# Second mixer of a two-block kernel: the first merge gate computed ahead of the second scan, and the scan's masked copies made by VectorE

## The reference, cut to what matters

```python
def merge_branches(gates, o_a, o_b, w_o_a, w_o_b, w_out):
    g_a, g_b = jnp.split(gates, 2, axis=-1)
    y = jax.nn.sigmoid(g_a) * (o_a @ w_o_a) + jax.nn.sigmoid(g_b) * (o_b @ w_o_b)
    return y @ w_out

def rwkv7_scan(r, w, k, v, a, b, s0):
    ...
    def step(s, inp):
        r_t, w_t, k_t, v_t, a_t, b_t = inp
        sa = jnp.einsum('...vk,...k->...v', s, a_t)
        s = s * w_t[..., None, :] + sa[..., :, None] * b_t[..., None, :] + v_t[..., :, None] * k_t[..., None, :]
        return s, jnp.einsum('...vk,...k->...v', s, r_t)
```

## Time and profile before

| | |
|---|---|
| runs | 2721.07 us median of 3 (2718.84 to 2724.94) |
| profiled execution | 2726.3 us, span from the first to the last instruction 2724.5 us |
| PE | 2413.0 us busy, 89% of the span; mean granted clock 0.946 |
| DVE, ACT, POOL | 893.3, 446.0, 85.5 us busy |
| DMA | 789.10 MB, mean 290 GB/s |

### The profile page before, as it was taken

One profiled execution on the slowest core, in us unless ns is written; L12 is line 12 of the kernel. 1 busy time (PEld: TensorE's weight loads), 2 busy tenths in 40 slices (PEclk: granted clock), 3 DMA queues, 4 the chain that ended last, 5 costly groups with the idle time before them and its releaser, 6 DMA issues. The chain is left out here.

```text
span 2724.5 us, 42972 instructions
## 1 busy us (share of the span) xinstructions
PE 2413.0 (89%) x19453; PEld 1308.2 (48%) x19453; DVE 893.3 (33%) x1682; ACT 446.0 (16%) x809; POOL 85.5 (3%) x93
## 2 busy tenths in 40 slices
PE   7999889899999999999999999896586899599985
PEld 4544343343433344434444443366576887355552
DVE  3225522303232222413141311374566521432222
ACT  3112101111111101211121201230041220000001
POOL 1001000000000000000010000000001100000000
PEclk9998879999999999999999999898797999699998
DMA  5356349999999999999999999830000033479996
GB/s 191 111 177 239 144 175 394 389 378 424 412 423 422 414 396 414 418 411 404 385 408 422 416 406 402 363 125 1 9 32 2 3 132 120 169 311 422 422 422 274
DMA packets 133522, 789.10 MB, mean 290 GB/s; under 512 B 17477, under 2 KB 27981, under 8 KB 69213
## 3 DMA queue, kind: packets, MB, share of 16 engines
q1 hardware_dynamic: 129885, 773.78, 70.3%
q0 software_dynamic: 3456, 12.58, 1.2%
HBM read 774.79 MB, written 11.53 MB: 289 GB/s over the span
## 5 line engine op out<-in xcount | busy, mean ns | idle before, releaser
L3090 PE MATMUL bank<-ring,arena 128*34 128x462 f32 (+1 forms) x3072 | 669.1, 572 | 68.0 <-DMA ring<-in_w_up 43.1
L3090 PEld LDWEIGHTS bank<-ring,arena 128*34 128x34 f32 x3072 | 175.2, 113 | 426.6 <-issue 406.3
L3113 PE MATMUL bank<-ring,arena 128*34 128x512 f32 (+1 forms) x1536 | 340.1, 559 | 0.6 <-DVE arena L2051 0.6
L3113 PEld LDWEIGHTS bank<-ring,arena 128*34 128x34 f32 x1536 | 101.7, 112 | 221.0 <-issue 203.6
L311 PE MATMUL bank<-arena,ring 128*128 128x256 f32 (+1 forms) x688 | 155.8, 388 | 3.7 <-ACT arena L1052 1.4
L311 PEld LDWEIGHTS bank<-arena,ring 128*128 128x128 f32 x688 | 131.7, 192 | 27.9 <-issue 2.0
L2044 DVE TENSOR_TENSOR arena<-arena,bank 34x462 f32<-34x462 f32 (+1 forms) x96 | 95.0, 1082 | 106.2 <-ACT arena L1121 105.9
L3569 PE MATMUL bank<-ring,arena 128*64 128x256 f32 x992 | 111.3, 380 | 6.9 <-DMA ring<-in_moe_w_up 6.1
L1121 ACT ACTIVATE arena<-bank 34x462 f32<-34x462 f32 (+1 forms) x96 | 84.9, 1038 | 121.1 <-PE bank L3090 120.9
L3569 PEld LDWEIGHTS bank<-ring,arena 128*64 128x64 f32 x992 | 73.5, 137 | 48.7 <-issue 17.0
L2988 PEld LDWEIGHTS bank<-arena 64*64 64x64 f32 x2304 | 73.1, 135 | 48.2 <-issue 47.8
(11 more groups left out here) (654 smaller groups left out, 2802.3 us busy)
## 6 DMA issues: line engine op xcount, KB each, us to landing
ring<-in_w_gate SPq DMA_DIRECT2D x128, 1408.0 KB, 13.1
ring<-in_w_up SPq DMA_DIRECT2D x128, 1408.0 KB, 12.8
ring<-in_w_down SPq DMA_DIRECT2D x128, 1408.0 KB, 10.7
ring<-in_w_in SPq DMA_DIRECT2D x47, 1024.0 KB, 7.2
ring<-in_moe_w_down SPq DMA_DIRECT2D x33, 1024.0 KB, 16.5
ring<-in_moe_w_gate SPq DMA_DIRECT2D x31, 1024.0 KB, 15.4
ring<-in_moe_w_up SPq DMA_DIRECT2D x31, 1024.0 KB, 17.9
ring<-in_ada_w SPq DMA_DIRECT2D x24, 1024.0 KB, 7.0
```

Of the source, the lines that this page charges most:

```text
L3090: last = mm(ps[c][row:row + CAP, 0:n], xsT[:, e, k, :], w[:, at:at + n], start=k == 0, stop=k == KT - 1)
L3113: last = mm(ps[6][row:row + CAP, c:c + n], hidT[:, j, :], w[:, at - m * PIECE:at - m * PIECE + n], start=j == 0, stop=j == FT - 1)
```

## The change

1. PE makes merge gate 0 as the last thing of the preparation, after the turning of v, into banks 0 and 1 (before: 6 and 7, in the merge). It waits first for both roots, which ACT reads from those banks. ACT takes its sigmoids (`merge_gates_act`) at the end of the same phase. The result lies in the free columns of ring slots 3 and 4 (`sgate_half`), so the scan's buffers are laid around these two slots (`in_ring`). SP loads the gate's two pieces behind the last two of the preparation, and the other 14 at the start of the merge.
2. POOL does nothing in the scan. DVE makes the first mask of `steps7` at the end of `start7_dve` for each direction, and the other four of both directions behind the two `pp` of level 0. PE waits for them in that order. (The scan of the context keeps its copies on POOL.)

```diff
@@ -686,6 +686,8 @@
 
         def in_ring(cols, shape, **names):
 
+            if spare[0] < 5 * PIECE and spare[0] + cols > 3 * PIECE:
+                spare[0] = 5 * PIECE
             v = ring[:, spare[0]:spare[0] + cols]
             spare[0] += cols
             assert spare[0] <= RING * PIECE
@@ -741,7 +743,9 @@
         lnx_eps = small[:, 47:48]
 
         A_COLS, B_COLS = 2064, 1920
-        sgate = [ar(4 * SEQ, "p (c t) -> p c t", c=4) for _ in range(4)]
+        sgate = [None] + [ar(4 * SEQ, "p (c t) -> p c t", c=4) for _ in range(3)]
+        sgate_half = lambda n, b: (sgate[n][:, 2 * b:2 * b + 2, :] if n else
+                                   ring[:, (3 + b) * PIECE + 4 * 512:(3 + b) * PIECE + 5 * 512].rearrange("p (c t) -> p c t", c=2))
         term = ar(4 * SEQ, "p (c t) -> p c t", c=4)
         merged = ar(KT * SEQ, "p (k t) -> p k t", k=KT)
         mod_row = ar(D)
@@ -753,6 +757,7 @@
         merge_out_pieces = [[piece((A["w_o_a_2"], A["w_o_b_2"])[br][:, g * 512:(g + 1) * 512].rearrange("(k p) c -> p k c", p=P),
                                    4 * 512, "p (k c) -> p k c", {"k": 4})] for g, br in MERGE]
         MERGE_BANKS = (6, 0, 2, 4)
+        assert [slot % RING for slot in (n_rwkv, n_rwkv + 1)] == [3, 4]
         w_out2_pieces = rows_pieces(A["w_out_2"])
         n_merge = len(pieces)
         sgate_ready, merge_read, m_row_filled, m_row_read, half_ready = (
@@ -904,10 +909,10 @@
             sp.wait_ge(phase_ended, 4 * N_PHASES_R)
             for dst, src in ((w2sb, A["rwkv_w2_2"]), (a2sb, A["rwkv_a2_2"])):
                 sp.dma_start(dst, src.rearrange("d r c -> (d r) c")).then_inc(w2_landed, up(w2_landed, 16))
-            issue(n_rwkv - 2, n_rwkv)
+            issue(n_rwkv - 2, n_rwkv + 2)
             sp.wait_ge(phase_ended, 4 * N_PHASES_R2)
             sp.dma_start(g2sb, A["rwkv_g2_2"]).then_inc(g2_landed, up(g2_landed, 16))
-            issue(n_merge - 16, n_merge)
+            issue(n_rwkv + 2, n_merge)
             sp.wait_ge(phase_ended, 4 * N_PHASES_M)
             for dst, src in ((router_w[:, :, 0:N_GRP], A["router_grp_2"].rearrange("(k p) e -> p k e", p=P)),
                              (router_w[:, :, N_GRP:LG], A["router_exp_2"].rearrange("(k p) e -> p k e", p=P)),
@@ -983,15 +988,6 @@
 
             pool.drain().then_inc(phase_ended, 1)
             pool.wait_ge(phase_ended, phase_end(pool))
-            pool.wait_ge(join7_landed, due(pool, join7_landed, 16))
-            for n in range(NCL):
-                for d in range(2):
-                    pool.wait_ge(ll_copied, due(pool, ll_copied))
-                    for s0, s1 in ((0, 1), (1, 5)):
-                        full = [P, s1 - s0, 4, C7]
-                        nc.gpsimd.tensor_tensor(steps7[d][:, s0:s1], ll[d][:, 1].unsqueeze(1).to_broadcast(full),
-                                                join7[:, 1 - d, s0 + 1:s1 + 1].unsqueeze(2).to_broadcast(full), ALU.mult).then_inc(steps7_ready, up(steps7_ready))
-                        pool.wait_ge(steps7_ready, own(pool, steps7_ready))
             pool.drain().then_inc(phase_ended, 1)
             pool.wait_ge(phase_ended, phase_end(pool))
             pool.drain().then_inc(phase_ended, 1)
@@ -1393,6 +1389,15 @@
             for c in range(NCL):
                 act.wait_ge(v7_filled, due(act, v7_filled))
                 ACTV(v7[:, c].rearrange("p q v -> p (q v)"), ps[4 + c][:, 0:SEQ], ACT.Copy)
+
+            def merge_gates_act(n, base):
+
+                act.wait_ge(piece_used, after(merge_gate_pieces[n]))
+                for b in range(2):
+                    last = ACTV(sgate_half(n, b).rearrange("p c t -> p (c t)"), ps[base + b][:, :], ACT.Sigmoid)
+                last.then_inc(sgate_ready, up(sgate_ready))
+
+            merge_gates_act(0, 0)
             act.drain().then_inc(phase_ended, 1)
             act.wait_ge(phase_ended, phase_end(act))
 
@@ -1445,11 +1450,8 @@
             ACTV(var7, var7, ACT.Sqrt, scale=1.0 / C7, bias=lnx_eps).then_inc(sqrt_ready, up(sqrt_ready))
             row_act(4, m5_row)
             row_act(6, mod_row)
-            for n in range(4):
-                act.wait_ge(piece_used, after(merge_gate_pieces[n]))
-                for b in range(2):
-                    last = ACTV(sgate[n][:, 2 * b:2 * b + 2, :].rearrange("p c t -> p (c t)"), ps[MERGE_BANKS[n] + b][:, :], ACT.Sigmoid)
-                last.then_inc(sgate_ready, up(sgate_ready))
+            for n in range(1, 4):
+                merge_gates_act(n, MERGE_BANKS[n])
             act.drain().then_inc(phase_ended, 1)
             act.wait_ge(phase_ended, phase_end(act))
             norm_act(act, x1, TILES2, xn2)
@@ -2313,6 +2315,13 @@
                     last.then_inc(dve_order, up(dve_order))
                     dve.wait_ge(dve_order, own(dve, dve_order))
                     TT(xx[d], id7.unsqueeze(1).unsqueeze(1).to_broadcast(full), xx[d], ALU.subtract).then_inc(x0_ready, up(x0_ready))
+                    masked_steps_dve(d, 0, 1)
+
+            def masked_steps_dve(d, s0, s1):
+
+                full = [P, s1 - s0, 4, C7]
+                TT(steps7[d][:, s0:s1], ll[d][:, 1].unsqueeze(1).to_broadcast(full),
+                   join7[:, 1 - d, s0 + 1:s1 + 1].unsqueeze(2).to_broadcast(full), ALU.mult).then_inc(steps7_ready, up(steps7_ready))
 
             def masks7_dve(n):
 
@@ -2342,6 +2351,8 @@
             for n in range(NCL):
                 for i in range(5):
                     level7_dve()
+                    for d in range(0 if i else 2):
+                        masked_steps_dve(d, 1, 5)
                 if n + 1 < NCL:
                     start7_dve(n + 1)
                 for d in range(2):
@@ -2389,7 +2400,7 @@
                 dve.wait_ge(sgate_ready, due(dve, sgate_ready))
                 dst = merged[:, 4 * g:4 * g + 4, :] if br == 0 else term
                 for b in range(2):
-                    last = TT(dst[:, 2 * b:2 * b + 2, :], sgate[n][:, 2 * b:2 * b + 2, :],
+                    last = TT(dst[:, 2 * b:2 * b + 2, :], sgate_half(n, b),
                               ps[MERGE_BANKS[n] + b][:, :].rearrange("p (c t) -> p c t", c=2), ALU.mult)
                 if br:
                     settled(last)
@@ -3304,6 +3315,19 @@
                 last.then_inc(turned, up(turned))
             pe.drain().then_inc(phase_ended, 1)
             pe.wait_ge(phase_ended, phase_end(pe))
+            def two_in_a_bank(pe, base, views, x):
+
+                for _, slot, count, _ in views:
+                    pe.wait_ge(slot, count)
+                kts = views[0][0].shape[1]
+                n = kts * len(views)
+                for ct in range(4):
+                    for k in range(n):
+                        last = mm(ps[base + ct // 2][:, ct % 2 * SEQ:(ct % 2 + 1) * SEQ],
+                                  views[k // kts][0][:, k % kts, ct * P:(ct + 1) * P], x[:, k, :], start=k == 0, stop=k == n - 1)
+                        if ct == 3 and k % kts == kts - 1:
+                            last.then_inc(piece_used, up(piece_used))
+
             def lows_pe(d):
 
                 ks = slice(64 * d, 64 * d + 64)
@@ -3339,6 +3363,8 @@
                         r = half7(h)
                         last = mm(ps[4 + c][r, q * C7:(q + 1) * C7], vT7[:, q, c * C7:(c + 1) * C7], ident[:, r], start=True, stop=True)
                 last.then_inc(v7_filled, up(v7_filled))
+            pe.wait_ge(root7, due(pe, root7, 2))
+            two_in_a_bank(pe, 0, merge_gate_pieces[0], u2x_lat)
             pe.drain().then_inc(phase_ended, 1)
             pe.wait_ge(phase_ended, phase_end(pe))
 
@@ -3396,7 +3422,7 @@
                     else:
                         pe.wait_ge(xx_copied, due(pe, xx_copied))
                     if i < 2:
-                        pe.wait_ge(steps7_ready, 4 * (4 + n) + 2 * d + 1 + i)
+                        pe.wait_ge(steps7_ready, 4 * (4 + n) + 2 * i + 1 + d)
                     for q in range(4):
                         for h in range(2):
                             r = half7(h)
@@ -3475,19 +3501,6 @@
             pe.wait_ge(s7_read, due(pe, s7_read, 2))
             pe.drain().then_inc(phase_ended, 1)
             pe.wait_ge(phase_ended, phase_end(pe))
-            def two_in_a_bank(pe, base, views, x):
-
-                for _, slot, count, _ in views:
-                    pe.wait_ge(slot, count)
-                kts = views[0][0].shape[1]
-                n = kts * len(views)
-                for ct in range(4):
-                    for k in range(n):
-                        last = mm(ps[base + ct // 2][:, ct % 2 * SEQ:(ct % 2 + 1) * SEQ],
-                                  views[k // kts][0][:, k % kts, ct * P:(ct + 1) * P], x[:, k, :], start=k == 0, stop=k == n - 1)
-                        if ct == 3 and k % kts == kts - 1:
-                            last.then_inc(piece_used, up(piece_used))
-
             def row_of_columns_pe(base, column):
 
                 for k in range(KT):
```

## The result

The change took 2681.72 us (median of 4 runs, 2675.1 to 2698.2) against 2723.01 us of the kernel before measured beside it: ratio 0.9867, 95% interval 0.9821 to 0.9913, that is 41 us less. The forecast was 2685.5 us, range 2678 to 2696.

The account below looks back on a forecast made before the run. PE was taken as the busiest engine, with time to win only where it idles, runs at low clock or can move work. 13.8 + 3 x 3.8 + 4.5 + 6.0 = 35.7 us off 2721.07 gave 2685.5 us, range 2678 to 2696.

Parts of the forecast that it names:

- Merge gate: Merge: gate 0's 64 instructions leave PE's stretch, -13.8 us; in the preparation they cost 0, with 2.7 us of cover.
- DVE's chain: Scan: without POOL's copies `start7_dve` shortens; -3.8 us at each of three chunk boundaries, -4.5 us in the first chunk.
- Large copies: Scan: DVE's 1024-column copies behind the first level's two `pp` cost 0, with 1.0 us of cover before PE needs them.
- Clock: Scan, level 0 and turning: PE at 2.4 GHz saves 2.4 us per chunk; between 0 and 9.6 us, 6.0 taken.
- Rival 1: Scan: the clock falls at every boundary all the same; gain 29.7 us, 2691.4 us; chance 0.24.
- Rival 2: Preparation: the gate is not hidden and the scan starts later; gain 21.9 us if wholly exposed, 2699.2 us; chance 0.05.
- Rivals 3 and 4: 3: long DVE rows are DVE's own, 26.7 us slower, chance 0.02; 4: scan gains nothing, gain 11.2 us, chance 0.04.

Follow-up runs that it names:

- gate_only: Against the kernel before, only merge gate 0 moved ahead of the scan, POOL keeping the scan's masked copies; ratio to before 0.9957, scan 154.0 us, merge 118.1 us.
- pool_reads: Against the changed kernel, POOL also makes the old masked copies, into unused columns that nobody reads; scan 154.8 us.
- copies_early: Against the changed kernel, DVE makes all five masks of a direction at the end of its half of `start7_dve`; scan 141.4 us, 10.4 more.

## Why the prediction was right

- **Merge gate:** -13.8 said, 13.9 measured in the merge, 0 in the preparation, with the 2.7 us of cover that were worked out. Right, and shown by *gate_only*. That the change's own merge comes out so near is in part luck, since two effects of the clock, 1.6 and 1.7 us, cancel in it. One reading was wrong: the merge does not end at 2330.3, for the product by `w_out` runs until 2334.48 (2305.05 and 29.43 us). The 108 us said for the merge, and the sign that one of over 110 would make the term wrong, go by that end. To the product's end it is 125.9 us before and 112.0 after, again 13.9 less.
- **DVE's chain:** 3.8 us per boundary said. From the start of `start7_dve` to the first `pp` it was 14.01 (2091.93 to 2105.94) and is 10.40 (2073.23 to 2083.63): 3.6. At the other two boundaries it was 14.0 and is 10.2: 3.8 each. In the first chunk 4.5 said, 4.4 measured (14.37 to 9.94 from DVE's last instruction of the preparation). Together 15.6, with 15.9 said. The choice of 0.43 us for L2312, against 0.64, was right: 416 to 426 ns.
- **Large copies:** cost nothing, as said; PE came for them 1.2 us after they were done (1.0 said), and at level 1 it does not wait for DVE.
- **Clock:** 6.0 us said, out of 0 to 9.6. From a chunk's first `pp` to the next `start7_dve` it was 23.0, 23.2 and 23.4 us and is 21.0, 21.0 and 22.6, and from the last first `pp` to the scan's end 28.0 and 25.6: 7.4 in all, which with the chain's 15.6 makes the scan's 23.0. The chunk whose boundary kept a low clock gave 0.8, the others 2.0 to 2.4. No row bore out the choice of 6.0 within its bounds, and that it came this near is luck in part. Level 0 and turning take 3.78 us at the full clock (2084.10 to 2087.88), 2.2 less and not 2.4. That the first products would stay at the low clock was right as well.
- **Rival 1** (the clock falls everywhere) was wrong at two boundaries of three. With the two short waits that are left the clock fell at one boundary of three. The Trainium skill, TensorE: Matmul & The Clock Gate, "HAM oscillation", describes a loop in which PE waits long for data in every turn and so starts every turn at the low clock. The longer waits of before agree: the clock fell at all three boundaries. The section does not treat waits as short as those after. **Rival 2**: no. **Rivals 3 and 4**: no, since without POOL's copies L2317 took 691 to 694 ns all eight times, and *pool_reads* brought the 1709 back. The row of DVE's products with a bank input, 414 to 422 ns throughout, had no weight here: none of them stood beside POOL's copies, which lie over L2312 and L2315 alone.
- The chances of the forecast and of rivals 1, 2 and 4 add up to 0.97, not to the 0.96 stated.
- The sum of the three stages was short by 1.2 us: 1.4 by the clock, 0.1 by the merge, less 0.3 by the chain. That the runs' median came out 41 us lower and not 37 is inside the interval (24 to 49 us).

## What to carry to other kernels

Before work is spread over a second engine, look at what the two share: here 27 us of POOL's work cost 16 us of DVE's chain and 7 more by the clock, and a product on the busy engine, under a stretch where it waits anyway, was free. Look for that stretch and put the large part there, since here 2.1 us per chunk in the wrong place cost 10 in four chunks. The changed kernel has one such place left: in the scan of the context, where POOL keeps its copies (L978), DVE's products of 512 columns (L1989) take up to 2790 ns where the shortest takes 692. No run moved those. Work that another stage's bound engine can do early is worth what it fills: the first gate fitted into 18 idle us and paid whole, the second had 4 left and paid 3 in the stages.

## What the runs showed of the hardware

- DVE's products with two SBUF inputs (256 and 512 columns) took 415 to 427 ns and 691 to 694 ns beside POOL's memsets of 1806 ns, the same as with POOL idle. With POOL's products in their stretch they took means of 1088 and 1709. In the scan of before every one of them that began under a POOL copy ended 0.28 us after it (256 columns) or 0.55 (512), so a POOL copy of 2.42 us made a DVE product of 0.43 us last up to 2.57. One that had begun 0.1 us ahead of the copy kept its 426 ns. DVE's products with one input in a bank (414 to 423 ns) never stood beside POOL's products in this scan, so no row shows what becomes of them there.
- A small change of PE's waits can move a stretch of low clock and so undo a gain: PE that came 1 us earlier through its first products met a longer wait and then ran level 0 at 0.55 in place of the products at 0.50. At the first boundary of *copies_early* PE waited 1.1 us more than in the change, and the scan's mean clock went from 0.97 to 0.93. But the waits alone do not settle it: at two boundaries of the changed kernel with the same waits (0.65 and 1.06 us) the clock fell at one and stayed full at the other.
